# Weight sums of nine down-projection jobs made by accumulating transfers instead of VectorE, the SiLU rows sent through memory, and the last two output tiles shared between engines

## What is computed

```python
D_MODEL, D_FF = 1024, 2816
sh1, sc1, gt1, sh2, sc2, gt2 = ada_mod(silu(c) @ w_ada + b_ada)      # once for c_ctx, once for c
h = modulate(rmsnorm(x, g_attn), sh1, sc1)
u = h @ w_in                                                         # q, k, v, gates
x = x + gt1 * merge_out(window_attention(u), neighbourhood_attention(u), gates)
x = x + gt2 * ((silu(h2 @ w_gate) * (h2 @ w_up)) @ w_down)           # h2 = modulated rmsnorm of x
```

## Time and profile before

| | before |
|---|---|
| time, median of 3 runs | 884.98 us (884.02 to 885.16) |
| the profiled execution's own time | 886.14 us |
| its span, first to last instruction | 884.3 us |
| TensorE busy | 873.2 us (99%) |
| VectorE busy | 704.9 us (80%) |
| ScalarE busy | 470.8 us (53%) |
| GpSimd busy | 122.2 us (14%) |
| DMA, mean over the span | 164 GB/s |

### The profile page before, as it was taken

One profiled execution on the slowest core, in us unless ns is written; L12 is line 12 of the kernel. 1 busy time (PEld: TensorE's weight loads), 2 busy tenths in 40 slices (PEclk: granted clock), 3 DMA queues, 4 the chain that ended last, 5 costly groups with the idle time before them and its releaser, 6 DMA issues. The chain is left out here.

```text
span 884.3 us, 16546 instructions
## 1 busy us (share of the span) xinstructions
PE 873.2 (99%) x6221; PEld 831.4 (94%) x6221; DVE 704.9 (80%) x1342; ACT 470.8 (53%) x980; POOL 122.2 (14%) x155
## 2 busy tenths in 40 slices
PE   7999999999999999999999999999999999999998
PEld 6698888888899999999999999999999999999997
DVE  4667998899788599773877869997777998777987
ACT  6663453777877523432256645554544555545543
POOL 0000000010000000000000132313433322333221
PEclk9999999999999999999999999999999999999999
DMA  9954433542452220328316398868989886898867
GB/s 364 390 221 167 144 118 121 172 129 73 148 167 85 73 72 1 117 75 357 97 38 223 74 204 188 179 162 213 202 189 202 185 184 171 195 204 189 181 152 147
DMA packets 51663, 145.32 MB, mean 164 GB/s; under 512 B 6000, under 2 KB 12416, under 8 KB 50176
## 3 DMA queue, kind: packets, MB, share of 16 engines
q1 hardware_dynamic: 32000, 102.38, 35.2%
q0 software_dynamic: 18864, 41.11, 24.2%
q10 hardware_dynamic: 720, 0.77, 0.2%
HBM read 121.68 MB, written 12.20 MB: 151 GB/s over the span
## 5 line engine op out<-in xcount | busy, mean ns | idle before, releaser
L1361 ACT ACTIVATE w_hi<-stage 128x512 fp32r<-128x512 f32 (+1 forms) x186 | 106.2, 608 | 90.9 <-DMA stage<-stage 45.0
L2083 DVE TENSOR_TENSOR w_lo<-stage,w_hi 128x512 fp32r<-128x512 f32 (+1 forms) x186 | 117.7, 667 | 20.0 <-ACT w_hi L1361 19.6
L2737 PE MATMUL ps<-m_hi,w_hi 128*128 128x320 f32 x304 | 93.9, 309 | 0.0
L2737 PE MATMUL ps<-m_lo,w_hi 128*128 128x320 f32 x304 | 93.9, 309 | 0.0
L2737 PE MATMUL ps<-m_hi,w_lo 128*128 128x320 f32 x304 | 93.9, 309 | 0.0
L2737 PE MATMUL ps<-h_hi,w_hi 128*128 128x320 f32 x272 | 84.1, 309 | 0.9 <-DVE w_lo L2083 0.9
L2737 PE MATMUL ps<-h_hi,w_lo 128*128 128x320 f32 x272 | 84.0, 309 | 0.0
L2737 PE MATMUL ps<-h_lo,w_hi 128*128 128x320 f32 x272 | 84.0, 309 | 0.0
L2737 PE MATMUL ps<-y_hi,w_hi 128*128 128x320 f32 x264 | 81.7, 309 | 0.0
L2737 PE MATMUL ps<-y_hi,w_lo 128*128 128x320 f32 x264 | 81.6, 309 | 0.0
L2737 PE MATMUL ps<-y_lo,w_hi 128*128 128x320 f32 x264 | 81.6, 309 | 0.0
(11 more groups left out here) (334 smaller groups left out, 2475.1 us busy)
## 6 DMA issues: line engine op xcount, KB each, us to landing
stage<-w_main SPq DMA_DIRECT2D x118, 512.0 KB, 4.2
x<-w_ada SPq DMA_DIRECT2D x21, 512.0 KB, 4.9
stage<-stage POOLq DMA_DIRECT2D x38, 256.0 KB, 5.0
qk<-w_ada SPq DMA_DIRECT2D x7, 1024.0 KB, 13.7
scr<-w_main POOLq DMA_DIRECT2D x28, 256.0 KB, 6.2
y_t<-scr POOLq DMA_DIRECT2D x22, 320.0 KB, 6.7
s_second<-w_main POOLq DMA_DIRECT2D x26, 256.0 KB, 5.9
stage<-w_main POOLq DMA_DIRECT2D x19, 256.0 KB, 6.5
```

The lines of the kernel that those rows point to most:

```text
L1361: act.activation(w_hi[:, slot, at:at + job_half(j) * P], left_stage(op, j), ACT.Copy).then_inc(left_hi[op], 1)
L2083: dve.tensor_tensor(w_lo[:, slot, w], left_stage(op, j), w_hi[:, slot, w].bitcast(F32), ALU.subtract).then_inc(left_lo[op], 1)
L2737: ins = pe.matmul(ps[:, BANK_OF[op], 0:TH], wt[:, slot, w], right(op, part, j, k), start=k == 0 and n == 0, stop=k == half - 1 and n == 2)
```

## The change

Four edits. One: `sums_by_vector` asks in addition that the job itself is a gate and up job, so the nine down jobs that follow a down job get S1, S2 and S4 from POOL's transfers, and S4 is split in the job that uses it. Two: the SiLU values are brought into 8 partitions by two small matmuls, copied by ScalarE, written to memory by ScalarE's queue and read back into `cbc` by a broadcast load on SyncE's queue, ahead of weight units 4 to 7; `silu_row` goes, and four matmuls of 512 columns on the arriving `x` (`keep_clock`) take its place. Three: in the last job ScalarE scales the first tile, POOL adds it to `kept[2]`, and VectorE's `last_tile` for it goes; SyncE's stores change their order. Four: at the start of the feed-forward phase `s1(1)` moves ahead of `s3_second_term(0)` and `s4(0)` on POOL.

```diff
 def sums_by_vector(j):
-    return j > 0 and JOBS[j - 1][1] is None
+    return j > 0 and JOBS[j - 1][1] is None and JOBS[j][1] is not None
...
+            c_rows = junk[0:KT, 0:2 * P]
...
                                      (ckb[:, :, :], cache_kb), (cvb[:, :], cache_vb)):
                         sp.dma_start(dst, src).then_inc(cache_in, 16)
+                    sp.wait_ge(cbc_out, 16)
+                    sp.dma_start(cbc, cbc_row.partition_broadcast(P)).then_inc(cbc_copied, 16)
...
             sp.wait_ge(last_done, 1)
+            sp.dma_start(y_t[:, KT - 1, TH:T], kept[3][:, TH:T]).then_inc(out_y, 16)
+            sp.wait_ge(pool_set, 5)
             sp.dma_start(y_t[:, KT - 2, :], kept[2]).then_inc(out_y, 16)
             sp.wait_ge(last_done, 2)
-            sp.dma_start(y_t[:, KT - 1, TH:T], kept[3][:, TH:T]).then_inc(out_y, 16)
-            sp.wait_ge(last_done, 3)
             sp.dma_start(y_t[:, KT - 1, 0:TH], kept[3][:, 0:TH]).then_inc(out_y, 16)
...
-            pool.wait_ge(cbc_copied, 2)
-            pool.dma_start(cbc_row, cbc[0:1, :]).then_inc(cbc_out, 16)
+            pool.wait_ge(cbc_copied, 16)
...
             s2(0)
+            s1(1)
             s3_second_term(0)
             s4(0)
-            s1(1)
             s3_first(1)
...
+            pool.wait_ge(rest_in, 32)
+            pool.wait_ge(r_done, 2 * down_number(len(JOBS) - 1) + 1)
+            nc.gpsimd.tensor_tensor(kept[2], kept[2], high_sb, ALU.add).then_inc(pool_set, 1)
...
-            for v, bank in ((0, 0), (1, 4)):
-                act.wait_ge(cbc_ready, v + 1)
-                act.activation(cbc[:, v * D_MODEL:(v + 1) * D_MODEL].rearrange("p (a b) -> p a b", a=2),
-                               ps[:, bank:bank + 2, :], ACT.Copy).then_inc(cbc_copied, 1)
+            act.wait_ge(cbc_ready, 1)
+            act.activation(c_rows, ps[0:KT, 0, 0:2 * P], ACT.Copy).then_inc(cbc_ready, 1)
+            act.wait_ge(cbc_ready, 2)
+            act.dma_start(cbc_row.rearrange("o (v j f) -> j (o v) f", v=2, f=P),
+                          c_rows.rearrange("j (v f) -> j v f", v=2)).then_inc(cbc_out, 16)
...
-                    ins = act.activation(kept[i][:, t], (low_sb if second else high_sb)[:, t], ACT.Identity,
+                    ins = act.activation((kept[i] if j + 1 < len(JOBS) else high_sb)[:, t],
+                                         (low_sb if second else high_sb)[:, t], ACT.Identity,
                                          scale=mod[:, g + kind:g + kind + 1])
...
-                elif more:
+                else:
                     scaled(j, 0)
...
-                else:
-                    last_tile(0, high_sb, slice(0, T)).then_inc(last_done, 1)
                 c22_u3(j)
...
-            def silu_row(v):
-                for j in range(KT):
-                    ins = pe.matmul(ps[:, (0, 4)[v] + j // 4, j % 4 * P:(j % 4 + 1) * P],
-                                    cpad[:, j, v:v + 1].to_broadcast([P, P]), ident, start=True, stop=True)
-                ins.then_inc(cbc_ready, 1)
-
-            silu_row(0)
-            silu_row(1)
+            for v in range(2):
+                ins = pe.matmul(ps[0:KT, 0, v * P:(v + 1) * P], cpad[:, :, v], ident, start=True, stop=True)
+            ins.then_inc(cbc_ready, 1)
+
+            def keep_clock(k):
+                pe.wait_ge(x_in[k], 16)
+                pe.matmul(ps[:, 6, 0:512], ident, x[:, k * T:k * T + 512], start=True, stop=True)
+
+            for n in range(4):
+                keep_clock(X_ORDER[n])
```

More of the change, by code:

```diff
@@ L1500, in ada_sum @@
                     dve.wait_ge(ada_dve, n)
+                elif not v:
+                    dve.wait_ge(cbc_copied, 16)
                 if n < ADA2_LATE:
@@ L2285, in ada_groups @@
                 pe.wait_ge(ada1_in[k % ADA1_SLOTS], 16 * (1 + k // ADA1_SLOTS))
-                if k == 2:
-                    pe.wait_ge(cbc_copied, 2)
-                elif k == 3:
+                if k == 3:
                     pe.wait_ge(rbc_done, 1)
@@ L2356, in first_block_k @@
                         if turn == 0:
-                            pe.wait_ge(cbc_copied, 1)
+                            pe.wait_ge(cbc_ready, 2)
                             pe.wait_ge(first_hi, 1)
```

## The result

| | before | after |
|---|---|---|
| median | 884.98 us | 904.34 us (900.47 to 912.06) |
| ratio | | 1.0229 [1.0204 to 1.0254] |
| profiled execution: time, span | 886.14, 884.3 us | 904.34, 902.5 us |
| first input-projection product | 19.03 us | 18.00 us |
| first product of the 31 jobs | 509.12 us | 508.11 us |

The change costs 20 us by the ratio; 5.8 were predicted, and the range ended at 896.0. The span grew by 18.2 us: the start is 1.0 shorter, the phase of the jobs 19.1 longer, the end 0.1 longer.

The account below looks back on a forecast made before the run. TensorE was taken to set the end, so only S4 halves later than their product cost time. 5.9 + 0.8 - 0.7 + 0.2 + 0 - 0.4 = +5.8 us on 884.98 gave 890.8 us, range 886.3 to 896.

Parts of the forecast that it names:

- The loop that decides the later jobs: Down jobs, A11's low half through S2's transfer and ScalarE and VectorE work to the next A11: 11.2 us per job.
- Parts 0 and 1: +0.8 us taken: Jobs 6 to 8 and 18 to 20 have more room, so cost 0.5 + 0.3 us, bounds 0 and 5.
- rival 1: Down jobs: transfers crowd each other and parts 0 and 1 stall too, +12.4 us, 897 us; chance 0.16.
- Later jobs have the loop of 11.2 ... so they gain room: Later down jobs of parts 0 and 1: loop of 11.2 us plus 0.4 fits in jobs of 12.32 us.
- 0.7 us from A11's low half to the issue of S2: Down jobs, on POOL: S2's transfer is issued 0.7 us after A11's low half ends, as in job 26.
- The landing of S2 behind both adds, taken at 6.0: Job 29: S2's transfer takes 6.0 us with both add_result transfers just ahead of it.
- The last part: +5.9 taken: Jobs 28, 29 and 30: stalls ahead of product S4 of 2.8, 1.9 and 1.2 us, bounds 1.1 and 10.
- split of S4 of job 30: Job 30: S4 split at about 881.9, its product due at 880.7, so a stall of 1.2 us.
- rival 4: TensorE's clock falls after each of three stalls in the last part, 1.5 us each: +10, 895 us; chance 0.06.
- the granted clock is 1.00 ... also after the gap at 528: TensorE before the change: clock at 1.00 in all windows, even after job 1's gap, 1.05 us; used against falling clocks.
- Edit four: -0.7 taken: Job 1: S1 issued some 3.6 us earlier may remove the 1.05 us gap; -0.7 us, bounds -1.05 and 0.
- Edit two's start: +0.2 taken: TensorE's start: keep_clock matmuls end 0.4 us after sum_columns begins now; +0.2 us taken, bounds -1.0 and +0.5.

Follow-up runs that it names:

- e3: The changed kernel with VectorE making the sums again in the last part only, parts 0 and 1 keeping the transfers: ratio 1.0132 [1.0110 to 1.0155].
- e1: The changed kernel with VectorE making S1, S2 and S4 of the nine down jobs again, the other three edits kept: ratio 1.0014 [1.0004 to 1.0024].
- e9: The changed kernel with 1536 bytes of scratch memory for POOL's DMA descriptors in place of 1024: ratio 1.0133 [1.0117 to 1.0148].
- e11: The changed kernel with unread matmuls filling the gaps ahead of S4 products, few enough that none should overrun: ratio 1.0174 [1.0153 to 1.0195].
- e15: The kernel before with edit two alone (SiLU rows through memory, keep_clock, early broadcast load): ratio 1.0033 [1.0020 to 1.0045].

## Why the prediction was wrong

The side was right, and so was the kind of loss: the stalls stand ahead of S4 products, ScalarE waits for stage transfers there, the gap of job 1 shrank to 0.63 us, `c22_u3` moved up as said. The time was 13.5 us off. The loop that decides the later jobs lacked a wait, and terms of the sum were mis-sized:

1. **Parts 0 and 1: +0.8 us taken, 10.4 measured** (e3 against e1). The traces have 8.0 (after: 6.3 of stalls, 1.7 of clock) and 10.6 (e3: 8.9 and 1.7). This was rival 1, with a chance of 0.16, and even it had only 4.8. The step that failed is "Later jobs have the loop of 11.2 ... so they gain room": from A11's low half to S4's low half it took 14.6 to 15.9 us in jobs 7, 8, 19 and 20, where the step makes it 12.1.
2. **What the loop left out.** It had 0.7 us from A11's low half to the issue of S2. That holds in the first jobs of a part, but behind the adds it was 3.2 to 4.0 us (1.0 in job 30), since POOL had no room to issue (e9). The trace before had 10.4 us of "issue" waits of POOL that I did not follow; with 27 transfers more they were 34.1. The landing of S2 behind both adds, taken at 6.0, was 5.5 to 6.8, so it was the wait for room and not the landing that the step had wrong.
3. **The last part: +5.9 taken, 8.6 measured.** The first stall was 3.6 (2.8), the second 1.3 (1.9), the third 3.1 (1.2): 7.9 us in the trace after, and 3.3 of clock. The 8.6 of the timed runs is uncertain by 3. By its own terms the prediction's split of S4 of job 30 comes to about 881.5, not 881.9, so to a stall of 0.8 and not 1.2.
4. **The clock: rival 4, chance 0.06.** It fell at each of the three longest stalls and cost 5 us (e11), where the rival had 4.5. The step "the granted clock is 1.00 ... also after the gap at 528" argued from a gap of 1 us about gaps of 3. And it was held as a rival to the stalls, though it comes with them: given stalls of 3 us it was no case of its own.
5. **Edit four: -0.7 taken, about -0.5 seen, not shown:** the gap is 0.6 us on average in ten traces with the edit (and 1024 bytes) and 1.1 in four without it, but it varies from 0 to 1.1 in the former and from 0 to 1.8 in the latter.
6. **Edit two's start: +0.2 taken, +0.3 to +0.4 found** at like rises of the clock, while the single pair of traces said -1.0. The broadcast load costs nothing: from the first product of the input projection to the first of the jobs it is 490.0 to 490.3 us in all traces, with it and without.
7. **Edit three: -0.4 taken, +0.1 to +0.6 in the traces.** The bounds had POOL's addition at up to 1.5 us (1.53 to 1.56 measured) but not that VectorE stands meanwhile.

One sum of the chances doesn't come out: the cases on the slower side add up to 0.88, not 0.86.

## What to carry to other kernels

Work moved off an engine that is not the bound onto a shared queue has to be priced as a loop: everything on that queue between one turn and the next, waits for room to issue included. "Issue" in the idle time of POOL's queue was room for descriptors near its limit here, and it stood in the profile before; that is the place to look before sending more through a queue. A stall that brings TensorE's clock down costs another 1.6 to 1.7 us, half as much again as the 2.5 to 3.6 us of the stalls here. And one pair of traces can't carry a claim of 1 us when the start of the same code scatters by 1.3; compare traces whose clock rose at the same moment.

## What the runs showed that I had not expected

- POOL had at most four transfers under way with 1024 bytes of descriptor memory and up to six with 1536; in a kernel with long stalls that was worth 1.0%, in the kernel before 0.1% with edit four.
- In the trace after, stalls of 1.8 us and less left the granted clock at 1.00, and at those of 2.5 us and more there was a stretch of over 3 us at 0.50; in other traces 1.7 and 1.9 us were enough, and 3.5 us were not. Useless matmuls in the gaps prevented it in both kernels that had them.
- An addition of 640 fp32 columns on POOL takes 1.53 to 1.56 us, and the VectorE operation with two operands in SBUF that runs beside it ends 0.35 us after it, in each of four traces.
- The load of `kept[3]` at the very end landed between 876.2 and 880.1 us in kernels whose last matmul began within 1.9 us of each other; in e15 it landed after the end of the last `c12` (878.5) and set the end.
